# Compression products in native fp32, four kernel rows on four 128x32 column tiles of the array, folded by one matmul

## The chip, the cores and the metric

The kernel runs on one NeuronCore of a Trainium2 chip. The time is the device time of one execution in microseconds (us), and a version is judged by the median of several runs. A NeuronCore has a matrix engine (TensorE, PE in the profile, with its weight loads shown apart as PEld), three engines for elementwise work (VectorE or DVE, ScalarE or ACT, GpSimd or POOL), and SyncE (SP), which here issues the loads of the weights. Each engine works through its own list of instructions in order and meets the others at semaphores.

## The reference

Two blocks run one after the other on 256 tokens of width 2048, everything in fp32. The first mixes a gated delta rule with block attention, the second mixes a compressed, a selected and a windowed attention. Nearly all the arithmetic is in large projections. The change touches one small part of the second block, the compression of keys and values:

```
def _compress(kv, pos_emb, w1, w2):            # kv: 256 tokens, 2 heads, 128 wide
    n_c = (S - CMP_BLOCK) // CMP_STRIDE + 1    # 15 blocks of 32 tokens, every 16
    idx = jnp.arange(n_c)[:, None] * CMP_STRIDE + jnp.arange(CMP_BLOCK)[None, :]
    blocks = kv[:, idx] + pos_emb[None, None, :, None, :]
    flat = blocks.transpose(0, 1, 3, 2, 4).reshape(B, n_c, Hkv, CMP_BLOCK * D)
    return jax.nn.silu(flat @ w1) @ w2         # w1: 4096 x 256, w2: 256 x 128
```

For the keys and again for the values, 30 rows (15 blocks of 2 heads) of length 4096 are multiplied with a matrix of 4096 x 256. Those 4096 are 32 "kernel rows" (the position in the block) of 128 numbers each.

## The kernel before

All weights are streamed once. They are cut into 396 pieces of 128 x 1024 fp32 (512 KB), and one piece is one *tick* of the program. SP loads a piece into one of five buffers `raw_w`. ACT rounds it to the reduced format fp32r (`hi_w`, `split` at L792) and DVE subtracts that from the original (`lo_w`, L1128); both do this two ticks ahead of the matmuls. PE (`products`, L1649) then multiplies in three passes of fp32r: high by high, high by low, low by high. A normal piece gives 12 matmuls with 512 moving columns (L1698). SP loads into a `raw_w` buffer once DVE has made the low part of its former piece (L621).

Between two pieces every engine does the small steps that a table (`PLAN`) puts at that tick: `rope_flip` transposes rotated queries or keys on PE and ACT copies them out, `att` n=0 makes scores, n=1 and 2 the softmax on DVE and ACT, n=3 transposes it on PE (copied by ACT, `att_p`), n=4 multiplies with the values. PE therefore alternates between a piece and a step.

The compression has 16 pieces of its own, eight for the keys (ticks 303, 305, 307, 309, 311, 313, 314, 315) and eight for the values (319, 321, 323, 325, 327, 329, 330, 331), each put between the normal pieces of a query projection. Such a piece holds four kernel rows of the 4096 x 256 matrix. The blocks with their position added (`blk`, L1511) are the stationary operand here and were also split once (`blocks_split`, L1038 and L1524) into `blk_parts`: high and low side by side, 60 columns. For each kernel row there are two matmuls with 256 moving columns (L1669), one of 60 stationary columns against `hi_w` and one of 30 against `lo_w`, all into the same 60 partitions of the accumulator. `cmp_rows` (L1043) copies these 60 rows out, `cmp_fold` (L1930) adds the two halves and transposes them with matmuls against a piece of the identity (L1936), and ACT applies silu to the result (L1050), which makes it load another function table, and another again for the exponentials of `att` that follow.

Of the kernel before, what the change touches and what calls it, by code (L numbers as in the profile page):

```python
# [152 lines left out]
def plan():  # L153
# [113 lines left out]
    for n, part in enumerate("kv"):  # L267
        at(END[("kcv",)] + 5 + n, "blocks", part)
        at(END[("kcv",)] + 6 + n, "blocks_split", part)
        at(END[("cmp", part)] + 1, "cmp_rows", part)  # L270
        at(END[("cmp", part)] + 2, "cmp_fold", part)
        at(END[("cmp", part)] + (6 if part == "k" else 4), "cmp_out", part)
# [41 lines left out]
def constants():  # L314

    i, j = np.arange(P)[:, None], np.arange(P)[None, :]
    f = np.float32
    out = {"ident": (i == j).astype(f), "upto": (i <= j).astype(f)}
    level = []
    for n in range(1, LEVELS + 1):  # L320
        m = 2 ** (n - 1)

        level.append(((i // (2 * m) == j // (2 * m)) & (j // m % 2 == 1) & (i // m % 2 == 0)).astype(f))
    below = (i > j).astype(f)
    out["levels"] = np.ascontiguousarray(np.stack([below, level[0].T] + level, 1))
    causal = np.where(j <= i, 0.0, NEG).astype(f)
    out["masks"] = np.ascontiguousarray(np.concatenate(
        [np.zeros((P, P), f), causal, np.where(j > i, 0.0, NEG).astype(f), causal], 1))
    s = np.arange(SEQ)
    ok = (np.arange(N_CMP) * 16 + 31)[None, :] <= s[:, None]  # L330
    cm = np.stack([np.where(ok, 0.0, NEG), ok.astype(f)], 1).astype(f)
    out["cmask"] = np.ascontiguousarray(cm.reshape(NT, P, 2, N_CMP).transpose(1, 2, 0, 3))
    rope = []
    for d in (128, 64):
        inv = f(10000.0) ** (-np.arange(0, d, 2, dtype=f) / f(d))
        ang = (s.astype(f)[:, None] * inv[None, :].astype(f)).astype(f).astype(np.float64)
        cos, sin = np.cos(ang), np.sin(ang)
        both = np.stack([np.concatenate([cos, cos], 1), np.concatenate([-sin, sin], 1)], 0).astype(f)
        rope.append(both.reshape(2, NT, P, d).transpose(2, 0, 1, 3))
    out["rope_a"], out["rope_b"] = (np.ascontiguousarray(r) for r in rope)  # L340
    return out


def build(nc, known, ins, out):

    ctx = ExitStack()
    with ctx:  # L347
# [29 lines left out]
        levels = place("levels", [P, LEVELS + 2, P], F32)  # L377
        masks = place("masks", [P, 2, SEQ], F32)
        cmask = place("cmask", [P, 2, NT, N_CMP], F32)
        rope_a = place("rope_a", [P, 2, NT, 128], F32)  # L380
# [98 lines left out]
        ob_tok = arena("ob_tok", [P, NT, 16 * 64], F32, 68)  # L479
        blk_parts = {p: arena(f"blk_parts_{p}", [P, CMP_L, 2, 2 * N_CMP], F32R, 16 + 8 * i) for i, p in enumerate("kv")}  # L480
        cmp_rows = arena("cmp_rows", [4 * N_CMP, 256], F32, 32)
        blk = {p: arena(f"blk_{p}", [P, CMP_L, 2, N_CMP], F32, 76 + 4 * i) for i, p in enumerate("kv")}
        qb_t = [arena(f"qb_t{i}", [P, QUAD, SEQ], F32, (8, 76)[i]) for i in range(2)]
# [121 lines left out]


        @block.sync
        def _(sp):
# [8 lines left out]
            def load(no):  # L617
                if no >= RAW_SLOTS:
                    old = no - RAW_SLOTS

                    sp.wait_ge(*lo_ready.after(old))  # L621
                sp.dma_start(piece_view(raw_w[no % RAW_SLOTS], no), piece_source(no)).then_inc(
                    *raw_ready[no % RAW_SLOTS].event(no))
# [12 lines left out]
            for n, (to, source) in enumerate(loads):  # L636
# [3 lines left out]
                (masks[:], ins["masks"].rearrange("p (a b) -> p a b", a=2)),  # L640
                (cmask[:], ins["cmask"]),
                (rope_a[:], ins["rope_a"]),
                (rope_b[:], ins["rope_b"]),
# [140 lines left out]
        def _(act):  # L784
# [7 lines left out]
            def split(no):  # L792

                slot = no % SPLIT_SLOTS
                act.wait_ge(*raw_ready[no % RAW_SLOTS].after(no))
                if no >= SPLIT_SLOTS:
                    act.wait_ge(*used.after(no - SPLIT_SLOTS))
                n = PIECES[no][2] * GROUPS[PIECES[no][0]].cols
                act.activation(hi_w[slot][:, 0:n], raw_w[no % RAW_SLOTS][:, 0:n], ACT.Copy).then_inc(  # L799
                    *hi_ready.event(no))  # L800
# [236 lines left out]

            def blocks_split(part):  # L1038
                act.wait_ge(*dve_did.after("blocks", part))
                act.activation(blk_parts[part][:, :, 0], blk[part][:].rearrange("p l i c -> p l (i c)"),  # L1040
                               ACT.Copy).then_inc(*act_did.event("blocks_hi", part))

            def cmp_rows_(part):  # L1043
                a = acc_of(END[("cmp", part)])
                act.wait_ge(*used.after(END[("cmp", part)]))
                if part == "v":
                    act.wait_ge(*pe_did.after("cmp_fold", "k"))
                act.activation(cmp_rows[:], a[0:4 * N_CMP, 0, 0:256], ACT.Copy).then_inc(*act_did.event("cmp_rows", part))

# [48 lines left out]
            for n in range(2):  # L1098
                for t in range(NT):
# [7 lines left out]
                     "gate_out": gate_out, "y_out": y_out, "head_gates": head_gates,  # L1107
                     "rope": rope, "rope_flip": rope_flip, "blocks_split": blocks_split, "cmp_rows": cmp_rows_,
                     "cmp_fold": cmp_fold, "cmp_out": cmp_out, "catt": catt,
# [10 lines left out]
        def _(dve):  # L1120
# [7 lines left out]
            def split(no):  # L1128

                slot = no % SPLIT_SLOTS  # L1130
                dve.wait_ge(*hi_ready.after(no))
# [63 lines left out]
            def ba_split():  # L1195
                dve.wait_ge(*act_did.after("ba_hi"))
                dve.tensor_tensor(ba_parts[:, :, 1], ba_raw[:, :, 0:16], ba_parts[:, :, 0].bitcast(F32),
                                  ALU.subtract).then_inc(*dve_did.event("ba_lo"))
                dve.wait_ge(*block2_rows.after(8))

# [310 lines left out]
            def blocks(part):  # L1511
# [4 lines left out]
                dve.wait_ge(*act_did.after("rope_flip", "kcv"))  # L1516
                s = kt2["kc" if part == "k" else "vc"][:].rearrange("p i (c l) -> p l i c", l=16)
                for n in range(2):
                    for i in range(2):
                        last = dve.tensor_tensor(blk[part][:, n * 16:(n + 1) * 16, i], s[:, :, i, n:n + N_CMP],  # L1520
                                                 over_cols(pos[part][:, n * 16:(n + 1) * 16], N_CMP), ALU.add)
                last.then_inc(*dve_did.event("blocks", part))

            def blocks_split(part):  # L1524
                dve.wait_ge(*act_did.after("blocks_hi", part))
                dve.tensor_tensor(blk_parts[part][:, :, 1], blk[part][:].rearrange("p l i c -> p l (i c)"),
                                  blk_parts[part][:, :, 0].bitcast(F32), ALU.subtract).then_inc(
                    *dve_did.event("blocks_lo", part))

# [56 lines left out]
            for n in range(2):  # L1586
                for t in range(NT):
# [8 lines left out]
                     "branch": branch, "y_out": y_out, "residual": residual, "head_gates": head_gates, "rope": rope,  # L1596
                     "blocks": blocks, "blocks_split": blocks_split, "catt": catt, "y_gate": y_gate, "y2_out": y2_out, "finish": finish}
            for tick in range(TICKS + LAST):
# [8 lines left out]
        def _(pe):  # L1607
# [41 lines left out]
            def products(no):  # L1649
# [8 lines left out]
                if group.kind == "cmp":  # L1658

                    hi, lo = (piece_view(w[no % SPLIT_SLOTS], no) for w in (hi_w, lo_w))  # L1660
                    parts = blk_parts[group.name[1]]
                    pe.wait_ge(*lo_ready.after(no))
                    pe.wait_ge(*dve_did.after("blocks_lo", group.name[1]))
                    for k in range(k0, k0 + n):
                        at_end = last and k == k0 + n - 1
                        both = ((4 * N_CMP, parts[:, k].rearrange("p b c -> p (b c)"), hi),
                                (2 * N_CMP, parts[:, k, 0], lo))
                        for m, (rows, x, w) in enumerate(both[::-1] if at_end else both):
                            i = pe.matmul(to[0:rows, 0, 0:256], x, w[:, k - k0], start=first and k == k0 and m == 0,  # L1669
                                          stop=at_end and m == 1)  # L1670
                    i.then_inc(*used.event(no))
# [258 lines left out]
            def cmp_fold(part):  # L1930
# [3 lines left out]
                for m in range(2):  # L1934
                    for b in range(2):
                        last = pe.matmul(aux[:, 0, m * 2 * N_CMP:(m + 1) * 2 * N_CMP], cmp_rows[:, m * P:(m + 1) * P],  # L1936
                                         ident[0:4 * N_CMP, b * 2 * N_CMP:(b + 1) * 2 * N_CMP], start=b == 0,
                                         stop=b == 1)
                last.then_inc(*pe_did.event("cmp_fold", part))
# [99 lines left out]
```

## Time and profile before

| | |
|---|---|
| median of 3 runs | 1315.29 us (1315.05 to 1315.99) |
| profiled execution, its own time | 1316.64 us |
| its span | 1314.8 us |
| PE busy | 1255.6 us, 95% of the span |
| PEld busy | 1085.6 us, 83% |
| DVE busy | 761.7 us, 58% |
| ACT busy | 615.5 us, 47% |
| PE, DVE, ACT busy from 1003.6 to 1091.3 us (the stretch of the compression pieces) | 84.2, 62.6, 53.4 of 87.7 us |

Busy time counts an instruction from its start to its end, and consecutive matmuls overlap: what a matmul costs is the distance from its start to that of the next. A native fp32 matmul stands in the trace as two records with a weight load each, an fp32r matmul as one. "128\*60 128x256" is a matmul with 128 rows and 60 columns of stationary operand and 256 moving columns.

### The profile page before, as it was taken

Reading aid. Unit: us, or ns where it says so; the run is one execution under the profiler, and the core shown is the slowest. Engines: PE = TensorE matmul, PEld = TensorE weight load, DVE = VectorE, ACT = ScalarE, POOL = GpSimd, SP = SyncE. Lnnn points to the kernel's source line nnn. Section 1 sums busy time; section 2 is a strip of 40 time slices with the busy share of each in tenths; the row PEclk is TensorE's granted clock in tenths of the full one; section 3 lists DMA queues with packets and bytes.
Section 4 is the critical chain, followed back from the end, with each engine's and each line's share of the span. In section 5 each row is a group of like instructions: output and inputs, shape, how many; then the busy total and the mean of one; then the engine's idle time right before and its main releaser. Section 6 shows DMA issues by size and latency. Waiting matters only on the chain. (4 is left out here: it accounts for less than half of the span.)

```text
span 1314.8 us, 17365 instructions
## 1 busy us (share of the span) xinstructions
PE 1255.6 (95%) x7040; PEld 1085.6 (83%) x7040; DVE 761.7 (58%) x976; ACT 615.5 (47%) x869; POOL 89.5 (7%) x126
## 2 busy tenths in 40 slices
PE   8999999995999999999999999799999999999996
PEld 6999988995988888888888888678888787878885
DVE  5668775652556646546454555477566766465553
ACT  4555445432223545543434344254445555466443
POOL 0100001197000000000000000000000000000000
PEclk9999999998999999999999999899999999999998
DMA  8646554563334654555566595355545655454662
GB/s 273 188 129 192 163 190 139 163 205 103 114 96 118 202 160 129 189 193 184 190 191 192 191 325 185 120 192 179 179 140 162 191 161 156 133 201 160 213 197 78
DMA packets 120705, 225.60 MB, mean 172 GB/s; under 512 B 9825, under 2 KB 21505, under 8 KB 119473
## 3 DMA queue, kind: packets, MB, share of 16 engines
q1 hardware_dynamic: 118386, 213.81, 51.7%
q0 software_dynamic: 2240, 10.68, 2.3%
q8 instruction: 56, 0.92, 0.3%
q14 instruction: 23, 0.19, 0.0%
HBM read 219.75 MB, written 4.72 MB: 171 GB/s over the span
## 5 line engine op out<-in xcount | busy, mean ns | idle before, releaser
L1133 DVE TENSOR_TENSOR lo_w<-raw_w,hi_w 128x1024 fp32r<-128x1024 f32 x396 | 482.1, 1229 | 373.5 <-ACT hi_w L799 372.3
L799 ACT ACTIVATE hi_w<-raw_w 128x1024 fp32r<-128x1024 f32 x396 | 411.1, 1057 | 263.5 <-PE acc L1698 208.0
L1698 PE MATMUL acc<-hi_w,h_hi 128*128 128x512 f32 (+1 forms) x832 | 330.9, 398 | 3.0 <-DVE h_lo L1141 2.7
L1698 PE MATMUL acc<-hi_w,h_lo 128*128 128x512 f32 (+1 forms) x832 | 322.2, 387 | 0.0
L1698 PE MATMUL acc<-lo_w,h_hi 128*128 128x512 f32 (+1 forms) x832 | 321.7, 387 | 0.0
L1689 PE MATMUL acc<-h_hi,hi_w 128*128 128x256 f32 x640 | 185.1, 289 | 1.3 <-DVE lo_w L1133 1.3
L1698 PEld LDWEIGHTS acc<-hi_w,h_hi 128*128 128x128 f32 x832 | 157.0, 189 | 34.8 <-issue 5.0
L1698 PEld LDWEIGHTS acc<-hi_w,h_lo 128*128 128x128 f32 x832 | 156.9, 189 | 32.5
L1689 PE MATMUL acc<-h_lo,hi_w 128*128 128x256 f32 x640 | 182.3, 285 | 0.0
L1689 PE MATMUL acc<-h_hi,lo_w 128*128 128x256 f32 x640 | 182.2, 285 | 0.0
L1698 PEld LDWEIGHTS acc<-lo_w,h_hi 128*128 128x128 f32 x832 | 157.2, 189 | 30.0 <-issue 0.7
L1689 PEld LDWEIGHTS acc<-h_hi,hi_w 128*128 128x128 f32 x640 | 124.1, 194 | 1.7 <-issue 1.6
L1689 PEld LDWEIGHTS acc<-h_lo,hi_w 128*128 128x128 f32 x640 | 124.2, 194 | 0.1
L1689 PEld LDWEIGHTS acc<-h_hi,lo_w 128*128 128x128 f32 x640 | 124.0, 194 | 0.0
L1698 PE MATMUL acc<-hi_w,m_hi 128*128 128x512 f32 x256 | 99.8, 390 | 0.0
L1698 PE MATMUL acc<-hi_w,m_lo 128*128 128x512 f32 x256 | 99.6, 389 | 0.0
L1698 PE MATMUL acc<-lo_w,m_hi 128*128 128x512 f32 x256 | 99.6, 389 | 0.0
L1698 PEld LDWEIGHTS acc<-hi_w,m_lo 128*128 128x128 f32 x256 | 48.0, 188 | 10.0
L1698 PEld LDWEIGHTS acc<-hi_w,m_hi 128*128 128x128 f32 x256 | 48.1, 188 | 9.9
L1698 PEld LDWEIGHTS acc<-lo_w,m_hi 128*128 128x128 f32 x256 | 48.1, 188 | 9.9
L954 ACT ACTIVATE att_s<-att_s,small 128x128 f32<-128x128 f32 (+1 forms) x80 | 35.5, 446 | 15.0 <-DVE small L1391 14.8
L1234 DVE SCALAR_TENSOR_TENSOR cv<-raw,conv_w,cv 128x255 f32<-128x255 f32 (+2 forms) x72 | 31.5, 479 | 3.9 <-ACT cv L861 3.0
(324 smaller groups left out, 1220.7 us busy)
## 6 DMA issues: line engine op xcount, KB each, us to landing
raw_w<-in_w_in SPq DMA_DIRECT2D x284, 512.0 KB, 3.7
raw_w<-in_w_out SPq DMA_DIRECT2D x64, 512.0 KB, 4.7
raw_w<-in_w_branch_a SPq DMA_DIRECT2D x16, 512.0 KB, 4.6
raw_w<-in_w_branch_b SPq DMA_DIRECT2D x16, 512.0 KB, 4.6
raw_w<-in_cmp_k_w SPq DMA_DIRECT2D x8, 512.0 KB, 4.4
raw_w<-in_cmp_v_w SPq DMA_DIRECT2D x8, 512.0 KB, 4.2
x_in<-in_x SPq DMA_DIRECT2D x4, 512.0 KB, 5.9
x<-in_x POOLq DMA_DIRECT2D x1, 2048.0 KB, 10.7
```

The source lines that it names most:

```text
L799: act.activation(hi_w[slot][:, 0:n], raw_w[no % RAW_SLOTS][:, 0:n], ACT.Copy).then_inc(*hi_ready.event(no))
L954: e = act.activation(att_s[:, i * k:(i + 1) * k], att_s[:, i * k:(i + 1) * k], ACT.Exp, bias=nmx[:, i:i + 1], scale=sc, accum_out=den[:, i ...
L1133: dve.tensor_tensor(lo_w[slot][:, 0:n], raw_w[no % RAW_SLOTS][:, 0:n], hi_w[slot][:, 0:n].bitcast(F32), ALU.subtract).then_inc(*lo_ready.e ...
L1234: last = dve.scalar_tensor_tensor(cv[:, i, back:SEQ], raw[:, i, 0:SEQ - back], conv_w[:, CONV - 1 - back, first + i:first + i + 1], cv[:, ...
L1689: i = pe.matmul(channels_of(no)[:, c], w[:, k, c * P:(c + 1) * P], x[:, k0 + k], start=first and c % 2 == 0 and k == 0 and m == 0, stop=la ...
L1698: i = pe.matmul(to[:, t, 0:group.cols], x[at], w[:, k], start=first and k == 0 and m == 0, stop=last and k == n - 1 and m == 2)
```

## The change

The compression pieces are no longer split, on ACT nor on DVE. PE multiplies the loaded `raw_w` itself in native fp32. The stationary operand is `blk`, now 32 columns per kernel row (30 and two of zeros), and kernel row k of a piece writes to the partitions 32k to 32k+31 of the accumulator, which places it on the k-th of four column tiles of the array. After eight pieces the 128 partitions hold four partial sums; `cmp_rows` copies 128 rows instead of 60, and `cmp_fold` adds the four and transposes them in one native matmul per half against a constant matrix `fold`. The buffer of such a piece becomes free when PE has used it, since no split reads it. `blocks_split` goes, on ACT and DVE.

```
-        at(END[("kcv",)] + 6 + n, "blocks_split", part)
...
+    out["fold"] = np.ascontiguousarray((i % 32 == np.arange(2 * N_CMP)[None, :]).astype(f))
...
+        def whole(no):
+            return GROUPS[PIECES[no][0]].kind == "cmp"
...
-                    sp.wait_ge(*lo_ready.after(old))
+                    sp.wait_ge(*(used if whole(old) else lo_ready).after(old))
...
+                (fold[:, 0:2 * N_CMP], ins["fold"]),
...
             def split(no):
+                if whole(no):
+                    return
...
-                act.activation(cmp_rows[:], a[0:4 * N_CMP, 0, 0:256], ACT.Copy).then_inc(*act_did.event("cmp_rows", part))
+                act.activation(cmp_rows[:], a[:, 0, 0:256], ACT.Copy).then_inc(*act_did.event("cmp_rows", part))
...
+                dve.memset(blk[part][:, :, 2 * N_CMP:32], 0.0)
...
-                    hi, lo = (piece_view(w[no % SPLIT_SLOTS], no) for w in (hi_w, lo_w))
-                    parts = blk_parts[group.name[1]]
-                    pe.wait_ge(*lo_ready.after(no))
-                    pe.wait_ge(*dve_did.after("blocks_lo", group.name[1]))
-                    for k in range(k0, k0 + n):
-                        at_end = last and k == k0 + n - 1
-                        both = ((4 * N_CMP, parts[:, k].rearrange("p b c -> p (b c)"), hi),
-                                (2 * N_CMP, parts[:, k, 0], lo))
-                        for m, (rows, x, w) in enumerate(both[::-1] if at_end else both):
-                            i = pe.matmul(to[0:rows, 0, 0:256], x, w[:, k - k0], start=first and k == k0 and m == 0,
-                                          stop=at_end and m == 1)
+                    w = piece_view(raw_w[no % RAW_SLOTS], no)
+                    pe.wait_ge(*raw_ready[no % RAW_SLOTS].after(no))
+                    pe.wait_ge(*dve_did.after("blocks", group.name[1]))
+                    for k in range(n):
+                        i = pe.matmul(to[32 * k:32 * (k + 1), 0, 0:256], blk[group.name[1]][:, k0 + k], w[:, k],
+                                      start=first, stop=last)
...
                 for m in range(2):
-                    for b in range(2):
-                        last = pe.matmul(aux[:, 0, m * 2 * N_CMP:(m + 1) * 2 * N_CMP], cmp_rows[:, m * P:(m + 1) * P],
-                                         ident[0:4 * N_CMP, b * 2 * N_CMP:(b + 1) * 2 * N_CMP], start=b == 0,
-                                         stop=b == 1)
+                    last = pe.matmul(aux[:, 0, m * 2 * N_CMP:(m + 1) * 2 * N_CMP], cmp_rows[:, m * P:(m + 1) * P],
+                                     fold[:, 0:2 * N_CMP], start=True, stop=True)
```

On PE, at the first compression piece of the keys (tick 303, between the transposes of `rope_flip` and the scores of `att`), the list of instructions read before:

```order
L1617 MATMUL aux<-ident,rot_165 128x128 x8
L1669 MATMUL acc<-hi_w_57,blk_parts_k 60x256
L1669 MATMUL acc<-lo_w_61,blk_parts_k 30x256
L1669 MATMUL acc<-hi_w_57,blk_parts_k 60x256
L1669 MATMUL acc<-lo_w_61,blk_parts_k 30x256
L1669 MATMUL acc<-hi_w_57,blk_parts_k 60x256
L1669 MATMUL acc<-lo_w_61,blk_parts_k 30x256
L1669 MATMUL acc<-hi_w_57,blk_parts_k 60x256
L1669 MATMUL acc<-lo_w_61,blk_parts_k 30x256
L1881 MATMUL aux<-kz,qb_t_161 128x256 x2
L1698 MATMUL acc<-hi_w_54,h_hi 128x512
```

and reads now (the sizes are those of the output):

```order
L1617 MATMUL aux<-ident,rot_164 128x128 x8
L1664 MATMUL acc<-raw_w_52,blk_k 32x256 x4
L1876 MATMUL aux<-kz,qb_t_160 128x256 x2
L1693 MATMUL acc<-hi_w_54,h_hi 128x512
```

Eight fp32r matmuls became four native ones, with the same neighbours on both sides.

On ACT, from the copy of `rope_flip` for `qb` at tick 302 to the copy of `att_p` two steps later, the list read before:

```order
L1027 ACTIVATE qb_t0_161<-aux 128x1024
L799 ACTIVATE hi_w1_55<-raw_w0_49 128x1024
L799 ACTIVATE hi_w2_56<-raw_w1_50 128x1024
L799 ACTIVATE hi_w3_57<-raw_w2_51 128x1024
L952 ACTIVATE small_74<-small_74 128x4
L954 ACTIVATE att_s_126,small_74<-att_s_126,small_74 128x128 x4
L799 ACTIVATE hi_w0_54<-raw_w3_52 128x1024
L961 ACTIVATE att_p_127<-aux 128x512
```

and reads now:

```order
L1034 ACTIVATE qb_t0_160<-aux 128x1024
L806 ACTIVATE hi_w2_56<-raw_w1_50 128x1024
L959 ACTIVATE small_75<-small_75 128x4
L961 ACTIVATE att_s_127,small_75<-att_s_127,small_75 128x128 x4
L806 ACTIVATE hi_w0_54<-raw_w3_52 128x1024
L968 ACTIVATE att_p_128<-aux 128x512
```

The two splits of compression pieces (`raw_w0`, `raw_w2`) are gone from ahead of the exponentials; DVE loses the matching two subtractions.

## Rows read from the trace of the kernel before

**Rows 1.** The page: engines; costliest groups (busy us, mean ns | idle before); loads (us to landing).

```profile
PE 1255.6 (95%) x7040; PEld 1085.6 (83%) x7040; DVE 761.7 (58%) x976; ACT 615.5 (47%) x869; POOL 89.5 (7%) x126
...
L1133 DVE TENSOR_TENSOR lo_w<-raw_w,hi_w 128x1024 fp32r<-128x1024 f32 x396 | 482.1, 1229 | 373.5 <-ACT hi_w L799 372.3
L799 ACT ACTIVATE hi_w<-raw_w 128x1024 fp32r<-128x1024 f32 x396 | 411.1, 1057 | 263.5 <-PE acc L1698 208.0
...
raw_w<-in_w_in SPq DMA_DIRECT2D x284, 512.0 KB, 3.7
```

**Rows 2.** Timeline of PE at tick 305 (start us, us from first start to last end).

```profile
1012.29 0.28 PE L1669 MATMUL acc<-hi_w,blk_parts_k 128*60 128x256 f32 x1
1012.41 0.28 PE L1669 MATMUL acc<-lo_w,blk_parts_k 128*30 128x256 f32 x1
...
1013.24 0.40 PE L1698 MATMUL acc<-hi_w,h_hi 128*128 128x512 f32 x1
```

**Rows 3.** Line L1669 alone (count: ns min/median/max, first and last start us).

```profile
L1669 PE MATMUL acc<-hi_w,blk_parts_k x32: 276/280/361, 1007.1 to 1037.7; 128*60 128x256 f32 x32
```

**Rows 4.** Groups by form on PE from 1007 to 1089 us: a native matmul of 256 columns.

```profile
L1888 PE MATMUL aux<-ks_t,qa_t 128*128 128x256 f32 x8 | 1.9, 379 | 0.0
```

**Rows 5.** Timeline around the fold of the values.

```profile
1096.84 1.03 PE L1617 MATMUL aux<-ident,rot 128*128 128x128 f32 x8
...
1097.80 1.07 PE L1936 MATMUL aux<-ident,cmp_rows 60*128 60x30 f32 x8
...
1098.81 0.50 PE L1698 MATMUL acc<-hi_w,h_hi 128*128 128x512 f32 x1
...
1099.14 0.39 PE L1698 MATMUL acc<-lo_w,h_hi 128*128 128x512 f32 x1
```

**Rows 6.** Timeline around the second compression matmul of the values (15 stationary columns).

```profile
1107.75 1.05 PE L1950 MATMUL aux<-w_v,hs_v 128*15 128x128 f32 x8
1108.72 0.41 PEld L1912 LDWEIGHTS aux<-vw_tok,att_p 128*128 128x128 f32 x3 [0.21 <-issue]
1108.73 0.49 PE L1912 MATMUL aux<-vw_tok,att_p 128*128 128x128 f32 x2
```

**Rows 7.** Waits of PE from 1007 to 1092 us (total us, times, longest).

```profile
PE aux L1617 <- ACT att_s L954: 2.5, 2, 2.3
PE aux L1912 <- ACT att_p L961: 0.4, 2, 0.2
PE aux L1881 <- ACT qb_t L1027: 0.3, 1, 0.3
PE acc L1698 <- DVE lo_w L1133: 0.2, 1, 0.2
```

**Rows 8.** Timeline of PE behind the piece of tick 311.

```profile
1028.23 0.28 PE L1669 MATMUL acc<-lo_w,blk_parts_k 128*30 128x256 f32 x1
1028.70 0.99 PE L1912 MATMUL aux<-vb,att_p 128*128 128x64 f32 x7 [0.19 <-ACT att_p L961]
```

**Rows 9.** Timeline: ACT from the copy of `rope_flip`, and PE's next transposes.

```profile
1047.39 1.02 ACT L1027 ACTIVATE qa_t<-aux 128x1024 f32<-128x1024 f32 x1 [6.53 <-PE aux L1617]
...
1048.43 1.28 ACT L1052 ACT_TABLE_LOAD   x1
...
1053.58 1.28 PE L1617 MATMUL aux<-ident,att_s 128*128 128x128 f32 x8 [2.27 <-ACT att_s L954]
```

**Rows 10.** The same transposes behind the values' fold.

```profile
1104.01 1.07 PE L1617 MATMUL aux<-ident,att_s 128*128 128x128 f32 x8 [2.19 <-ACT att_s L954]
```

**Rows 11.** Busy time by stretch: after the columns of the engines PEclk, DMA share, GB/s.

```profile
1054.30:1057.70 3.40, 3.40 (x19) 3.22 (x17) 2.02 (x2) 2.89 (x4) 0.00 (x0) 0.50 0.20 40
1104.00:1107.40 3.40, 3.39 (x19) 2.98 (x20) 1.51 (x2) 2.79 (x3) 0.00 (x0) 1.00 0.10 16
```

**Rows 12.** Timeline: load of tick 310 and the splits of 309 to 311.

```profile
1010.66 0.37 SPq L622 DMA_DIRECT2D raw_w<-in_w_in  x1
...
1017.10 2.94 ACT L799 ACTIVATE hi_w<-raw_w 128x1024 fp32r<-128x1024 f32 x3
```

More of the change, by code:

```diff
@@ L378, in build @@
         masks = place("masks", [P, 2, SEQ], F32)
+        fold = place("fold", [P, 32], F32)
         cmask = place("cmask", [P, 2, NT, N_CMP], F32)
@@ L479, in build @@
         ob_tok = arena("ob_tok", [P, NT, 16 * 64], F32, 68)
-        blk_parts = {p: arena(f"blk_parts_{p}", [P, CMP_L, 2, 2 * N_CMP], F32R, 16 + 8 * i) for i, p in enumerate("kv")}
-        cmp_rows = arena("cmp_rows", [4 * N_CMP, 256], F32, 32)
-        blk = {p: arena(f"blk_{p}", [P, CMP_L, 2, N_CMP], F32, 76 + 4 * i) for i, p in enumerate("kv")}
+        cmp_rows = arena("cmp_rows", [P, 256], F32, 32)
+        blk = {p: arena(f"blk_{p}", [P, CMP_L, 32], F32, 76 + 4 * i) for i, p in enumerate("kv")}
         qb_t = [arena(f"qb_t{i}", [P, QUAD, SEQ], F32, (8, 76)[i]) for i in range(2)]
@@ L1036, in rope_flip @@
                 i.then_inc(*act_did.event("rope_flip", *name))
[L1038 to L1041, printed above, removed]
             def cmp_rows_(part):
@@ L1107, in _ @@
                      "gate_out": gate_out, "y_out": y_out, "head_gates": head_gates,
-                     "rope": rope, "rope_flip": rope_flip, "blocks_split": blocks_split, "cmp_rows": cmp_rows_,
+                     "rope": rope, "rope_flip": rope_flip, "cmp_rows": cmp_rows_,
                      "cmp_fold": cmp_fold, "cmp_out": cmp_out, "catt": catt,
@@ L1128, in split @@
             def split(no):
+                if whole(no):
+                    return
                 slot = no % SPLIT_SLOTS
@@ L1198, in ba_split @@
                                   ALU.subtract).then_inc(*dve_did.event("ba_lo"))
-                dve.wait_ge(*block2_rows.after(8))
+                dve.wait_ge(*block2_rows.after(9))
             def r1_row_():
@@ L1517, in blocks @@
                 s = kt2["kc" if part == "k" else "vc"][:].rearrange("p i (c l) -> p l i c", l=16)
+                dve.memset(blk[part][:, :, 2 * N_CMP:32], 0.0)
                 for n in range(2):
                     for i in range(2):
-                        last = dve.tensor_tensor(blk[part][:, n * 16:(n + 1) * 16, i], s[:, :, i, n:n + N_CMP],
+                        to = blk[part][:, n * 16:(n + 1) * 16, i * N_CMP:(i + 1) * N_CMP]
+                        last = dve.tensor_tensor(to, s[:, :, i, n:n + N_CMP],
                                                  over_cols(pos[part][:, n * 16:(n + 1) * 16], N_CMP), ALU.add)
                 last.then_inc(*dve_did.event("blocks", part))
[L1524 to L1528, printed above, removed]
             def catt(t, n):
@@ L1596, in _ @@
                      "branch": branch, "y_out": y_out, "residual": residual, "head_gates": head_gates, "rope": rope,
-                     "blocks": blocks, "blocks_split": blocks_split, "catt": catt, "y_gate": y_gate, "y2_out": y2_out, "finish": finish}
+                     "blocks": blocks, "catt": catt, "y_gate": y_gate, "y2_out": y2_out, "finish": finish}
             for tick in range(TICKS + LAST):
```

## Prediction

> **What bounds the kernel now.** I read the page first: PE is busy for 95% of the span, DVE 58% and ACT 47% [rows 1], so a microsecond taken from DVE or ACT counts only where PE waits for it. Next I read PE's timeline at one compression piece. The reader is to see distances between starts, not durations: eight matmuls of 256 columns follow each other every 0.118 us, from 1012.29 to the next piece's start at 1013.24, 0.95 us in all, and nothing is lost at either edge [rows 2]. There are 64 such matmuls for the keys (32 high, and as many low) and 64 for the values [rows 3], so the 16 pieces hold PE for about 15 us. Last I read PE's waits in this stretch: 3.4 us in six waits, of which 2.3 is one long one behind the fold of the keys [rows 7], and a like one of 2.19 us follows the fold of the values [rows 10]. All waits but the long one follow a compression piece or a normal piece whose `lo_w` came late. The idle column counts from the modelled end of the last matmul, so the delay is larger than it says: behind tick 311 the starts are 0.47 us apart where 0.12 is usual, a loss of 0.35 [rows 8]. Read so (start to start, in the same timeline), the five waits behind compression pieces (ticks 303, 311, 314, 327, 330) cost 0.43, 0.35, 0.38, 0.35 and 0.23 us, and the two for `lo_w` (ticks 316 and 332) about 0.35 each; the waits view leaves out the last of the five and the first of the two, since their idle part is under its threshold.
>
> **Streaming of a piece.** The nearest row for a native fp32 matmul of 256 columns is L1888: eight records take 1.9 us from first start to last end and one lasts 0.379, so they start every (1.89 - 0.38)/7 = 0.216 us [rows 4], using 1.89 from the timeline that rounds to this 1.9. Two records are one matmul, 0.43 us, against 0.118 for a pass of fp32r. A changed piece has four native matmuls, eight records. What a piece costs then hangs on how far the column tiles work at the same time, which no row of this trace shows: every matmul here writes from partition 0 on. The bounds are: one after the other, 8 x 0.216 = 1.73 us; all four tiles at once, 2 x 0.216 and a few ns, 0.44 us. Between these lies what I expect. PE starts its matmuls in the order of its list, and the two records of one native matmul use the same tile and stand next to each other. The second must wait 0.216 us for the first; the next tile's first record can start beside it, but that tile's second must wait again. So the records pair up like stairs, five steps of 0.216 = 1.08 us. I take this, +0.13 us per piece, 16 pieces, **+2.1 us**.
>
> By the Trainium skill (TensorE: Matmul & The Clock Gate, Part 3) matmuls start and end strictly in program order, and a group packed on several tiles spans one matmul plus about 4 ns per tile. The first half gives my stairs; the second, read without regard to the two records, gives 0.44 us per piece and the rival below.
>
> **Going to the tiles and back.** Where PE changes from a full-size matmul to one on part of the array, the trace shows a price. Into the fold (60 of 128 rows) the starts are 0.96 us apart for eight records of 0.109 us, 0.09 too long; its own eight take 1.01 us at 0.112 each, 0.1 too long by its end; and the matmul behind it has its successor 0.33 us later where 0.23 is usual, 0.1 more [rows 5]. With 15 of 128 columns in native fp32 it is the same: 0.98 us for eight records of 0.109, and the weight load behind it could not run ahead (idle 0.21) [rows 6]. So one round trip costs 0.3 us. The old 60- and 30-column matmuls in fp32r paid none [rows 2]. The 16 pieces make 14 round trips, since nothing of PE's stands between ticks 313 and 314, nor 329 and 330: **+4.2 us**.
>
> The Trainium skill (TensorEngine Tiling (Array Packing), Key Properties) says that a change of tiling mode drains TensorE; the rows above give the price.
>
> **Waits that absorb.** The five waits behind compression pieces end with ACT's copy or exponential, not with PE. PE comes there 0.13 + 0.19 us later (the longer piece, the way in, and the drain), so it waits 0.32 less, or down to nothing: 4 x 0.32 + 0.23 = **-1.5 us**. (At 1.73 us per piece they vanish, -1.75; at 0.44 they grow by 0.32 each, +1.6.)
>
> **Relief of DVE and ACT.** Sixteen splits go: 16 x 1.06 = 17 us of ACT and 16 x 1.23 = 20 us of DVE [rows 1]. PE waited for `lo_w` twice with a loss of 0.35 each, behind three compression pieces in a row: **-0.7 us**. The rest was hidden behind PE and is worth nothing. `blocks_split`, 1.0 us on ACT and 1.2 on DVE twice, lies under unbroken projection matmuls of `qa`, as do the two small memsets that come instead.
>
> **The fold.** Half of its records go and it now uses all 128 rows: 0.45 + 0.3 = 0.75 us less of PE, twice. But behind it PE has one normal piece and then waits for an exponential whose chain on ACT begins with the copy of `rope_flip` before the fold and goes straight on: the copy ends at 1048.41 and the table load starts at 1048.43, silu, table, exponentials [rows 9]. The fold, finished by 1048.4, is no later than that copy. So PE's 2.27 us become 3.0, and 2.19 become 2.9 [rows 9, 10]: 0. That is if the clock stays. Behind the first of these gaps the granted clock was 0.50 for 3.4 us, which is the 1.2 GHz level, behind the second it was 1.00 [rows 11]; half speed for 3.4 us costs 1.7. With longer gaps it may fall behind both or neither, +-1.7 us in the range, 0 in the sum.
>
> **Loads.** A `raw_w` buffer of a compression piece is now freed by PE and not by DVE, some 2.5 us later, and SP's queue is in order, so every later load waits too. Tightest is tick 310: its load went at 1010.66, and would go when PE ends tick 305, at 1013.24; with 3.7 us to landing [rows 1] that is 1016.9. ACT split tick 310 as the second of three at 1018.1 [rows 12], so 1.1 us remain, and PE took the piece only at 1023.7, 5.6 us later than ACT. Cost 0. The one added constant takes half a microsecond of SP's queue at the start, ahead of a load that landed two microseconds before ACT took it: 0.
>
> **Sum.** 2.1 + 4.2 - 1.5 - 0.7 = +4.1 us on the profiled execution's 1316.64, 1320.7. The profiled one stands 1.35 above the median of the runs; on that median, 1315.29, it is **1319.4 us**, +0.31%.
>
> **Rivals.** All go by the same sum with another streaming time.
> (1) All four tiles at once, 0.44 us a piece: 16 x (-0.51) = -8.2, +4.2, +1.6, -0.7 = -3.1, **1312.2 us**. For it: the order of starts alone doesn't forbid it if the tiles' two records can wait independently. Against it: the adjacent records of one matmul stand 0.216 apart in every row. The sum crosses zero at about 0.72 us per piece; below that the kernel is faster.
> (2) No overlap: native fp32 on column tiles runs one after the other, so the change doesn't do what it says: 16 x 0.78 = 12.5, +4.2, -1.75, -0.7 = +14.2, **1329.5 us**. For it: in every row of native fp32 a record starts only when the one before has streamed.
> (3) Stairs, and the clock falls behind both gaps: +4.1 + 1.7, **1321.1 us**. Longer idle speaks for it, one of two gaps without a fall against.
> (4) Loads come late after all: if landing took over 6 us in the stretch, ACT would split later by 1 us at some ticks. DVE and ACT have over 5 us of lead over PE there, so 1321 at most.
>
> **How the numbers follow.** Stairs at a steady clock count 0.34, and with (3) and (4) 0.44; (2) 0.28; (1) 0.23; something else 0.05. A difference under 0.2% (2.6 us) cannot be told from no change on this kernel. Stairs lie above that except where the clock gets better (0.08 of the 0.44 go to same). (1) at -0.24% sits on the edge, half faster and half same. So faster 0.14, same 0.22, slower 0.64. The range goes from (1) to (2), since leaving either out would leave out more than 2 in 10: 1312 to 1330. The stairs' own range is 1317.5 to 1321.5.
>
> **What would show it.** Starts of the eight records within a piece: pairs a few ns apart every 0.216 us (right), all in two bunches (1), or an even 0.216 (2). From first record to the next full-size matmul: 1.17 us, and 0.1 more behind it. Waits for `qb_t`, `att_p` and `att_s` behind compression pieces near zero, none for `lo_w` at ticks 316 and 332, the two long gaps at 2.9 to 3.0 us. I am wrong if a round trip costs much less than 0.3 with column tiles, or if the tiles don't pair.

## The result, and the profile after

The changed kernel takes **1318.5 us** (median of 20 runs, 1316.9 to 1322.02), the kernel before 1316.26 us in the same comparison (20 runs, 1314.62 to 1318.1): ratio **1.002**, 95% interval 1.0013 to 1.0026. The forecast was 1319.4 us. The number is nearly right; the difference is less so: +4.1 us was forecast and +2.2 us measured (interval 1.7 to 3.4), and the kernel before is itself 1.0 us above the median on which the forecast stands. The sum behind the number is wrong in two places that work against each other: the stretch where the change works got faster, about as the forecast's rival (1) says, and matmuls that the change never mentions got slower.

The profiled execution of the changed kernel took 1322.02 us, span 1319.8; it is the longest of its 20 runs, so sizes below are taken from distances between starts, not from its end.

First the place of the change. PE's timeline at one compression piece (tick 305), which answers to [rows 2]:

```profile
1019.36 0.39 PE L1693 MATMUL acc<-hi_w,h_lo 128*128 128x512 f32 x1
1019.68 0.64 PE L1664 MATMUL acc<-raw_w,blk_k 128*32 128x256 f32 x8
1020.25 0.50 PE L1693 MATMUL acc<-hi_w,h_hi 128*128 128x512 f32 x1
1020.59 0.39 PE L1693 MATMUL acc<-lo_w,h_hi 128*128 128x512 f32 x1
```

The piece's eight records fill 0.64 us from first start to last end, where one alone lasts 0.38 to 0.40. The same piece as a group of its own records (count: ns min/median/max, first and last start us):

```profile
L1664 PE MATMUL acc<-raw_w,blk_k x8: 379/391/403, 1019.7 to 1019.9; 128*32 128x256 f32 x8
```

All eight start between 1019.7 and 1019.9. In the single records there are two bunches: 1019.68, .69, .70, .70, and then 1019.92, .93, .94, .94. That is the first pass of all four column tiles, 6 to 7 ns apart, and 0.24 us later the second pass of all four. The next full-size matmul starts 0.57 us after the first record, where the forecast said 1.17 and the old piece took 0.95. The price of going to the tiles and back stands beside it as forecast: 1019.36 to 1019.68 is 0.32 where 0.23 is usual, 1020.25 to 1020.59 is 0.34 where 0.23 is usual, and 0.57 less the 0.46 of streaming leaves 0.11: 0.3 us.

PE's waits from 1000 to 1115 us, for [rows 7] and [rows 10]:

```profile
PE aux L1617 <- ACT att_s L961: 5.9, 2, 3.0
PE aux L1907 <- ACT att_p L968: 1.6, 3, 0.5
PE aux L1876 <- ACT qb_t L1034: 0.6, 1, 0.6
```

The two long gaps are 3.0 and 2.9 us, `lo_w` is gone from the list, and the waits for `att_p` and `qb_t` grew instead of vanishing, because PE comes there earlier. Between the start of tick 303 and that of tick 332 the changed kernel gains 4.5 us on the one before (from 1014.61 to 1094.30 us, against 1007.13 to 1091.27). Not all of that is the change. In the kernel before, a fall of the granted clock to 0.50 [rows 11] covers the piece of tick 319 and the step behind it; from the start of the piece to that of the scores behind the step it takes 4.23 us there:

```profile
1054.51 0.56 PE L1669 MATMUL acc<-hi_w,blk_parts_v 128*60 128x256 f32 x1
1058.74 1.11 PE L1888 MATMUL aux<-ks_t,qa_t 128*128 128x128 f32 x8
```

and 3.19 us in the last kernel of the experiments below, which has the same piece and step at a granted clock of 1.00:

```profile
1052.55 0.36 PE L1671 MATMUL acc<-hi_w,blk_parts_v 128*60 128x256 f32 x1
1055.74 1.11 PE L1890 MATMUL aux<-ks_t,qa_t 128*128 128x128 f32 x8
```

So about 1.0 of the 4.5 us is the clock, and some 3.4 us are left for the change.

Now matmuls that the change doesn't touch, those of 512 columns as groups (busy us, mean ns of one | idle before). The second name is the tile held in the array, the stationary operand. In the kernel before:

```profile
L1698 PE MATMUL acc<-hi_w,h_lo 128*128 128x512 f32 x800 | 313.1, 391 | 0.0
L1698 PE MATMUL acc<-hi_w,m_hi 128*128 128x512 f32 x256 | 99.8, 390 | 0.0
L1698 PE MATMUL acc<-hi_w,ob_hi 128*128 128x512 f32 x64 | 24.9, 389 | 0.0
```

And after:

```profile
L1693 PE MATMUL acc<-hi_w,h_lo 128*128 128x512 f32 x800 | 314.2, 393 | 0.0
L1693 PE MATMUL acc<-hi_w,m_hi 128*128 128x512 f32 x256 | 101.2, 395 | 0.0
L1693 PE MATMUL acc<-hi_w,ob_hi 128*128 128x512 f32 x64 | 25.3, 395 | 0.0
```

Each record from `m` and `ob` lasts 5 to 6 ns longer. Records overlap, so the distance between starts decides: in PE's timeline at the last projection, twelve matmuls take 2.72 us before (1290.05 to 1292.77):

```profile
1290.05 0.39 PE L1698 MATMUL acc<-hi_w,m_hi 128*128 128x512 f32 x1
...
1292.77 0.39 PE L1698 MATMUL acc<-hi_w,m_hi 128*128 128x512 f32 x1
```

and 2.79 us after (1290.02 to 1292.81):

```profile
1290.02 0.39 PE L1693 MATMUL acc<-hi_w,m_hi 128*128 128x512 f32 x1
...
1292.81 0.39 PE L1693 MATMUL acc<-hi_w,m_hi 128*128 128x512 f32 x1
```

Over all of them the mean distance is 226.7 ns before and 232.4 ns after. This holds for every matmul of 512 columns whose stationary operand lies in the working area (`oa`, `ob`, `m`: 192 + 192 + 768 = 1152), and for none from `h_hi` or `h_lo`. 1152 x 5.7 ns = **6.6 us**. What the change did to them is one line of the diff: `fold`, 128 bytes a partition, was placed ahead of `cmask`, so that all tiles behind it, the working area too, lie 128 bytes higher, while `hi_w`, `lo_w` and `h` stay.

### The profile page after: what moved, and what is told of

Same layout as the page of the kernel before. It is cut to its first block and busy times, and to the rows that moved or that the text cites. A ratio compares the mean times of both kernels' runs of the same rounds, so it can differ in the third digit from the quotient of the medians.

```text
span 1319.8 us, 17300 instructions
## 1 busy us (share of the span) xinstructions
PE 1256.6 (95%) x7032; PEld 1073.9 (81%) x7032; DVE 741.8 (56%) x960; ACT 598.4 (45%) x851; POOL 89.5 (7%) x126
## 5 line engine op out<-in xcount | busy, mean ns | idle before, releaser
L1137 DVE TENSOR_TENSOR lo_w<-raw_w,hi_w 128x1024 fp32r<-128x1024 f32 x380 | 462.8, 1229 | 381.7 <-ACT hi_w L806 380.3
L806 ACT ACTIVATE hi_w<-raw_w 128x1024 fp32r<-128x1024 f32 x380 | 395.6, 1056 | 279.1 <-PE acc L1693 221.9
```

The lines of the kernel that those rows point to most:

```text
L1137: dve.tensor_tensor(lo_w[slot][:, 0:n], raw_w[no % RAW_SLOTS][:, 0:n], hi_w[slot][:, 0:n].bitcast(F32), ALU.subtract).then_inc(*lo_ready.e ...
```

## The experiments

Kernels that went to the same chip share its runs of the kernel before, whose median there was 1316.27, 1317.47 and 1315.65 us for the three groups below. Ratios are to those, with 95% intervals.

### Where the lost time is

The changed kernel with the constant somewhere else:

```diff
-        fold = place("fold", [P, 32], F32)
...
+        fold = arena("fold", [P, 32], F32, 106.5)
```

> The changed kernel, with its constant `fold` placed above the working area (at 106.5 KB from its start), so that nothing else moves from where it was before the change. Placement theory: the 1152 matmuls of 512 columns whose stationary operand lies in the working area (oa, ob, m) start 226.7 ns apart again and not 232.4, 1152 x 5.7 ns = 6.6 us, so 1318.5 - 6.6 = 1311.9 us, below both kernels; their records last 389 to 390 ns and not 395. Rival, that the time is lost in the pieces, their round trips or the clock and not by the placement: 1318.5 us, records still 395 ns.

Measured: 1313.51 us (12 runs), ratio 0.9979 (0.9967 to 0.9991); 5.0 us less than the changed kernel (5.4 by the two ratios) for moving one constant, where 6.6 were expected. The records are back at

```profile
L1693 PE MATMUL acc<-hi_w,m_hi 128*128 128x512 f32 x256 | 99.8, 390 | 0.0
```

and the distance at 226.7 ns. The placement theory holds, and the change without its side effect is faster than the kernel before by 2.8 us (interval 1.2 to 4.3). Part of this can be the clock: the mean granted clock of its 12 runs is 0.9850, that of the 29 runs of the kernel before 0.9838, and 0.0012 of 1316 us is 1.6 us, an estimate of the most that it can be. Then the reverse, the shift without the change:

```diff
+        place("unused", [P, 32], F32)
         cmask = place("cmask", [P, 2, NT, N_CMP], F32)
```

> The kernel before, with an unused tile of 128 bytes a partition ahead of `cmask`, so that the working area moves by 128 bytes and nothing else changes. Placement theory: 1316.3 + 6.6 = 1322.9 us, the matmuls from oa, ob and m at 232.4 ns, those from h_hi and h_lo at 226.7. Rival (placement is free): 1316.3 us.

Measured: 1324.92 us (5 runs), ratio 1.0058 (1.0045 to 1.0071), 8.7 us more between the medians and 7.6 by the ratio, interval 5.9 to 9.3. The matmuls from `m` take the same step:

```profile
L1699 PE MATMUL acc<-hi_w,m_hi 128*128 128x512 f32 x256 | 101.2, 395 | 0.0
```

Their mean distance is 232.4 ns. Those from `h` stay at 227.4 to 228.0, which they have in the kernel before too. Two more falls of the clock than in the profile of the kernel before (3.4 us at half speed each, at 393.8 and 1110.6) may be the rest of the 8.7. Next 256 bytes (`[P, 64]` in the same place), and then all tiles moved together:

> The kernel before, with the working area moved by 256 bytes. If the place within 256 bytes counts: 1316.3 us, all at 226.7 ns. If any other distance from the weights' buffers or a larger period counts: about 1322.9 us or more.

Measured: 1317.17 us (11 runs), ratio 1.0003 (0.9994 to 1.0011); 226.7 ns. The second:

```diff
-        cursor = [start]
+        cursor = [start + 128]
```

> The kernel before, with every tile moved by 128 bytes, the weights' buffers too, so that no distance between two operands changes. If the distance between the stationary and the moving operand counts: 1316.3 us, all at 226.7 ns. If the place of one operand by itself counts: the 2400 matmuls of 512 columns from h_hi and h_lo slow down too, 3552 x 5.7 ns = 20.2 us, 1336.5 us, and up to 5.5 us more if the 1920 matmuls of 256 columns lose half as much each.

Measured: 1316.48 us (11 runs), ratio 1.0001 (0.9992 to 1.0009); all at 226.7 ns. So moving everything costs nothing, and 128 bytes cost what 256 bytes do not: what counts is how far operands lie apart, counted modulo 256 bytes (in the kernel before, the buffers, `h` and the working area all start at multiples of 256 bytes from one another). Then 64 bytes (`[P, 16]`):

> The kernel before with its working area moved by 64 bytes. 0 and 256 bytes cost nothing, 128 bytes 8.6 us. If the cost grows evenly with the distance to the next multiple of 256: half, about 1320.6 us, starts 229.6 ns apart. If only the 128-byte half counts: 1316.3 or 1324.9 us. If any misfit costs the same: 1324.9 us.

Measured: 1324.73 us (6 runs), ratio 1.0055 (1.0039 to 1.007); distance 233.4 ns. Half the shift costs no less than the whole, so the cost does not grow with it. Last, one of the four kinds of operand alone:

```diff
+        place("unused0", [P, 32], F32)
         lo_w = [place(f"lo_w{i}", [P, PIECE_KT * COLS], F32R) for i in range(SPLIT_SLOTS)]
+        place("unused1", [P, 32], F32)
```

> The kernel before, with the four `lo_w` buffers alone moved by 128 bytes (all behind them by 256). If the misfit is one between the two operands of a matmul: those of `lo_w` with h_hi, oa_hi and m_hi alone go from 226.7 to about 232.4 ns, 1184 x 5.7 = 6.7 us, 1323.5 us or some more if the 640 of 256 columns lose too; those of `hi_w` stay at 226.7. If it is one of the working area with something else (transfers into `raw_w`, the writes of ACT and DVE): no matmul changes, about 1316.8 us.

Measured: 1332.06 us (4 runs), ratio 1.0121 (1.0106 to 1.0135). The rival is out, since now the matmuls from `h` slow down as well; but my size was wrong by more than two, because the cost does not stay with the matmuls of `lo_w`. PE's timeline in a projection from `h`:

```profile
900.11 0.40 PE L1700 MATMUL acc<-hi_w,h_lo 128*128 128x512 f32 x1
900.34 0.39 PE L1700 MATMUL acc<-hi_w,h_hi 128*128 128x512 f32 x1
900.57 0.39 PE L1700 MATMUL acc<-lo_w,h_hi 128*128 128x512 f32 x1
...
902.88 0.40 PE L1700 MATMUL acc<-hi_w,h_lo 128*128 128x512 f32 x1
```

Twelve distances make 2.77 us, 231 ns each. Over the whole trace those that end at a start of `lo_w,h_hi`, `hi_w,h_lo` and `hi_w,h_hi` are 234.1, 232.5 and 230.9 ns, where the kernel before has 227.8, 227.4 and 227.9: 14.4 ns for three, 11.5 us for 800 such threes. The 384 threes from `oa`, `ob` and `m` lose 16.6 to 19.9 ns each, some 6.8 us. That makes 18 us; the runs say 16.4, interval 13.9 to 17.8. The 1920 matmuls of 256 columns lose nothing: their distances go from 119.8 to 119.1 ns, which gives back 1.3 us. Each of the three neighbours in the list is touched, so the misfit is not one of a matmul's own two operands only. Which pair of reads collides stays open.

### What the column tiles do

All four kernel rows on one column tile, `fold` on top:

```diff
-                        i = pe.matmul(to[32 * k:32 * (k + 1), 0, 0:256], blk[group.name[1]][:, k0 + k], w[:, k],
-                                      start=first, stop=last)
+                        i = pe.matmul(to[0:32, 0, 0:256], blk[group.name[1]][:, k0 + k], w[:, k],
+                                      start=first and k < 1, stop=last and k >= 3)
```

(The copy and the fold then take 32 rows.)

> The changed kernel with `fold` on top (1313.5 us), and all four kernel rows of a piece on the first column tile, summed in PSUM. If different tiles overlap and one tile does not: 8 x 0.216 = 1.73 us of streaming a piece instead of 0.46, 16 x 1.27 = 20.3 us, less some 3.3 us of waits behind pieces that vanish, so 1330.5 us, with eight even starts 0.216 us apart. Rival, that the bunches come from the 32 columns alone and not from the four tiles: 1313.5 us with bunches as before.

Measured: 1331.57 us (4 runs), ratio 1.0111 (1.0092 to 1.0129). Starts within the piece are 0.215 to 0.217 us apart, behind a first distance of 0.24. With two column tiles (`to[32 * (k % 2):...]`, kernel rows 2 and 3 added to 0 and 1):

> As the run before, but kernel rows 0 and 2 on the first column tile, 1 and 3 on the second. If the tiles run at once and one tile's records one after the other: four bunches of two, 4 x 0.216 = 0.88 us a piece, 16 x 0.42 = 6.7 us, less about 2 us of waits that shrink: 1318.2 us. If the order of the list holds (stairs): pairs of the second pass of one with the first pass of the next, seven steps or so, 1.3 us a piece or more, 1325 us.

Measured: 1319.23 us (10 runs), ratio 1.0016 (1.0004 to 1.0028). The three pieces side by side, each behind transposes of `att_s` or `rot`; one tile, then two, then four:

```profile
1016.62 1.91 PE L1664 MATMUL acc<-raw_w,blk_k 128*32 128x256 f32 x8
```

```profile
1015.00 1.06 PE L1664 MATMUL acc<-raw_w,blk_k 128*32 128x256 f32 x8
```

```profile
1017.88 0.64 PE L1664 MATMUL acc<-raw_w,blk_k 128*32 128x256 f32 x8
```

Less one record's 0.38 these are 1.53, 0.68 and 0.26 us from first to last start. With two tiles the records start at 1005.54, .54, then .78, .78, then .99, 1006.00, then 1006.21, .22: four bunches of two. The two passes of one matmul wait for each other, and so do two matmuls on one tile; matmuls on different tiles start 7 ns apart. The stairs of the forecast are in no trace.

The price of a round trip by itself. The run with one column tile, but as a full-size matmul:

```diff
-                        i = pe.matmul(to[0:32, 0, 0:256], blk[group.name[1]][:, k0 + k], w[:, k],
+                        i = pe.matmul(to[:, 0, 0:256], blk[group.name[1]][:, k0:k0 + n].rearrange("p k c -> p (k c)"), w[:, k],
```

> As the run with one column tile (1331.6 us), but each matmul takes all four kernel rows of the piece as a stationary operand of 128 columns and writes 128 partitions, so that the same eight records of 256 columns run on the full array (the sums then mix kernel rows: this changes what is computed). If the price of 0.3 to 0.4 us a round trip is that of column tiles: 14 x 0.4 = 5.6 us less, 1326 us, starts into and out of a piece at usual distances. If it is that of native fp32 behind fp32r: 1331.6 us.

Measured: 1325.69 us (4 runs), ratio 1.0072 (1.0059 to 1.0086). From the start of tick 303 to that of 332 it takes 4.3 us less than the run with one column tile, with one fall of the clock in each: 4.3 / 14 = 0.30 us a trip. Its piece and what follows:

```profile
1018.23 0.60 PE L1617 MATMUL aux<-ident,att_s 128*128 128x128 f32 x4
1018.66 1.89 PE L1664 MATMUL acc<-raw_w,blk_k 128*128 128x256 f32 x8
1020.39 1.00 PE L1907 MATMUL aux<-vb,att_p 128*128 128x64 f32 x8
```

Four transposes take 0.43 us to the piece and the piece 1.73 to the next matmul; with one column tile it is 0.52 and 1.85:

```profile
1016.10 0.60 PE L1617 MATMUL aux<-ident,att_s 128*128 128x128 f32 x4
1016.62 1.91 PE L1664 MATMUL acc<-raw_w,blk_k 128*32 128x256 f32 x8
1018.47 0.77 PE L1907 MATMUL aux<-vb,att_p 128*128 128x64 f32 x5
```

So native fp32 itself costs nothing to go to; using 32 of the 128 columns does. (The matmuls of the kernel before with 60 and 30 columns, in fp32r, paid nothing [rows 2], so the price is shown for native fp32 only.) In the single records the way in takes 0.203 us with one column tile and 0.109 at full width, the next matmul starts 0.310 us behind the piece's last record against 0.215, and its successor comes up to 0.11 late.

### What the fold's shortening is worth

In both kernels the fold's gain was hidden by the long gaps, which end with exponentials behind two table loads and a silu on ACT. So I moved those away, with `fold` on top:

```diff
-        at(END[("cmp", part)] + 2, "cmp_fold", part)
+        at(END[("cmp", part)] + 3, "cmp_fold", part)
...
+    for part in "kv":
+        at(END[("cmp", part)] + 3, "cmp_silu", part)
...
-                     "cmp_fold": cmp_fold, "cmp_out": cmp_out, "catt": catt,
+                     "cmp_silu": cmp_fold, "cmp_out": cmp_out, "catt": catt,
```

(The last two lines are in ACT's table of steps; the new step is planned behind those of the attention, so that ACT takes it after the tick's copy of `att_p`.)

> The changed kernel with `fold` on top (1313.5 us), and each part's fold one tick later on PE, its silu on ACT behind that tick's copy of `att_p`, so that the two table loads and the silu (2.8 us) no longer stand ahead of the exponentials that PE waits for. If the two long gaps (3.0 and 2.9 us) are these: both go to near zero, 1313.5 - 5.9 = 1307.6 us. Rival: the silu now holds the bank that the next scores take, or the table loads hold the next copy, and the wait comes back there: 1310 to 1313.5 us.

Measured: **1306.87 us** (5 runs, 1305.73 to 1307.9), ratio 0.9918 (0.9903 to 0.9933), the fastest of all. ACT's timeline:

```profile
1049.78 1.02 ACT L970 ACTIVATE att_p<-aux 128x1024 f32<-128x1024 f32 x1 [0.30 <-PE aux L1619]
1050.82 1.28 ACT L1056 ACT_TABLE_LOAD   x1
1052.12 0.22 ACT L1056 ACTIVATE hs_k<-aux 128x60 f32<-128x60 f32 x1
```

and PE's:

```profile
1048.00 0.52 PE L1932 MATMUL aux<-fold,cmp_rows 128*128 128x30 f32 x4
1048.68 1.06 PE L1619 MATMUL aux<-ident,att_s 128*128 128x128 f32 x8 [0.16 <-ACT att_s L963]
```

The gap of 3.0 us is 0.16, and the one behind the values' fold is 0.05. A smaller one came in their place: the second table load now stands ahead of the exponentials of a later tick (at 1057.96 us, behind `ck_t`), and PE waits for those:

```profile
1061.05 0.63 PE L1619 MATMUL aux<-ident,att_s 128*128 128x128 f32 x4 [0.53 <-ACT att_s L963]
```

The normal piece ahead of it takes 3.50 us from its start to these transposes, where it takes 2.82 in the run with `fold` on top. So the rival was right for 0.7 us. In the traces, from tick 303 to tick 336, the edit gains 5.2 us (98.99 to 93.84), which is the forecast 5.9 less this 0.7. The medians differ by more, 6.6 us, but they are from two chips. The same edit in the kernel before:

> The kernel before with the same move of the fold and the silu as in the run that took 1306.9 us, and nothing else. If the change's fold (0.75 us shorter, twice) was worth nothing only because the long gaps hid it, it now counts: this kernel is 3.1 + 1.5 = 4.6 us slower than that one, 1311.5 us. If the fold is hidden by something else as well: 1310 us.

Measured: 1311.29 us (6 runs), ratio 0.9966 (0.9953 to 0.9978). From tick 303 to tick 336 it takes 98.78 us, the one with column tiles 93.84; the clock falls in neither. The 4.9 us between them are near the 4.6 expected, but not all of it is what was expected. One wait stands in this kernel alone, at the step behind the piece of tick 321, where VectorE is late with the scores' maximum:

```profile
1061.05 0.63 PE L1949 MATMUL aux<-hs_k,w_k 128*128 128x30 f32 x4 [0.50 <-DVE small L1393]
```

It costs 0.66 us from start to start (the piece takes 1.61 to the next step instead of 0.94). The two folds are worth 1.0 us here and not 1.5: each is over 0.7 us shorter, but PE then comes to the exponentials before they are done, and 0.41 us of the first and 0.55 of the second count. That leaves 3.3 us for the pieces, their round trips and waits. So the fold's gain was indeed hidden by the long gaps, for two thirds of its size, and that the sum came out at 4.6 is partly luck.

## Why the prediction was right or wrong

**Streaming of a piece (+2.1 us): wrong, the step that failed first.** I wrote that the second record of a native matmul must wait 0.216 us and that "the next tile's first record can start beside it, but that tile's second must wait again", hence five steps. The waiting is as said, but it is the tile's own: the first passes of all four tiles go out 7 ns apart, before the second pass of any. Two steps, 0.24 us between the bunches as measured and 0.22 for the second to stream (the distance of one record to the next in the run with one tile), make 0.46 and not 1.08: **-7.8 us** in place of +2.1. The rows I argued from all had consecutive records on the full array, where the two rules look the same. By the Trainium skill (TensorE: Matmul & The Clock Gate, Part 3) a packed group spans one matmul plus about 4 ns a tile; the trace agrees, with 6 to 7 ns, and I gave the reading from the list's order more weight than this one, which was rival (1) with a chance of 0.23.

**Round trips (+4.2 us): right.** 14 x 0.30, measured by the run at full width against the one at 32 columns.

**Waits that absorb (-1.5 us): wrong in sign, and only because streaming was.** For 0.44 us a piece the prediction had +1.6. The waits for `att_p` and `qb_t` behind pieces went from 0.7 us in [rows 7] to 2.2 (from 1000 to 1115 us the kernel before has 0.7 too). The modelled ends hide more: with `fold` on top, the piece that starts at 1017.88 is followed at 1018.64, 0.76 us later, by a matmul that needs ACT's copy, which ends at 1018.59, and the idle column shows nothing. From start to start in the changed kernel (a piece without a wait takes 0.57 us to the next matmul, two in a row 1.00) the five waits that the forecast names cost 0.71, 0.62, 0.17, 0.62 and 0, together 2.1 us where they cost 1.7, and four more pieces (ticks 307, 315, 323, 331) take 0.19 to 0.21 us longer than 0.57. That is about +1.2 us.

**Relief of `lo_w` (-0.7 us): right in direction, and mis-sized.** Both ticks still start late; only the idle parts fell below what the waits view lists. The start of tick 332 comes 0.48 us behind the last record of the step before it, and it was 0.57:

```profile
1093.83 0.38 PE L1883 MATMUL aux<-kw_t,qa_t 128*128 128x256 f32 x1
1094.30 0.47 PE L1693 MATMUL acc<-hi_w,h_hi 128*128 128x512 f32 x1
```

(before: 1090.70 and 1091.27 us). `lo_w` of this piece is done at 1094.17 us, 0.13 before that start. At tick 316 the same distance went from 0.70 to 0.54. That is 0.25 us gained in all.

**The fold (0): right, and the reason shown.** The gaps are the forecast 3.0 and 2.9 us. With ACT's table loads out of the way the two folds are worth 1.0 us.

**Loads (0): right, with less to spare than I said.** The load of tick 310 went out at 1020.38, and ACT split it at 1024.35, right behind its landing at 1024.33; PE took the piece at 1030.51, 6.2 us later.

**Clock (0 in the sum): within the 1.7 us allowed, and to the good.** Where the granted clock was 0.50 behind the keys' gap in [rows 11], it is 1.00 behind both gaps now (stretch, then PE, PEld, DVE, ACT and POOL busy, PEclk, DMA share, GB/s):

```profile
1059.26:1062.70 3.44, 2.90 (x27) 2.25 (x28) 1.48 (x3) 2.77 (x3) 0.00 (x0) 1.00 0.19 35
1107.03:1110.50 3.47, 3.47 (x20) 2.97 (x20) 1.59 (x2) 2.77 (x3) 0.00 (x0) 1.00 0.11 16
```

although the gaps grew. That is the 1.0 us above. All five profiles of the kernel before or of it merely shifted by 64 to 256 bytes show one or two such falls of 3.4 us between 1050 and 1115 us, as does the run with `lo_w` moved; none of the three profiles with four column tiles does, but neither does that of the kernel before with fold and silu moved. Two of these four have no long gap left, so there no fall is missing. In the other two, the changed kernel and the one with `fold` on top, a gap of 3.0 us is followed by none, and why stays open. In the profiled execution of the changed kernel the clock also stood at half for 6.8 us from 392.5, which the one before has not (392 to 400 us, PEclk 0.57):

```profile
392.00:400.00 8.00, 7.51 (x26) 6.39 (x27) 4.45 (x6) 0.00 (x0) 1.30 (x2) 0.57 0.18 53
```

A fall of 3.4 us at this place (392 to 394 us) stands in the profiles of three of the shifted or edited versions of the kernel before, too, so it is not the change that makes the clock fall there. At half speed 6.8 us cost up to 3.4 us, about the 3.5 by which that execution is above its median; that this is the whole reason is not shown.

**The missing term (+6.6 us).** The change part by part ended, in the prediction, with what each operation costs. One edit was costed by its transfer alone: "the one added constant takes half a microsecond of SP's queue at the start ... 0". It also moved every tile behind it. The sum as it should have been: rival (1), -3.1, plus 6.6, makes +3.5 us, and +2.2 was measured. On 1315.29, the median that the forecast had, this gives 1318.8 us; on 1316.26, the median of the comparison, 1319.8, against 1318.5 measured. The 1.3 us are not accounted for. The kernel with the constant on top, -3.1 on 1316.27 = 1313.2, took 1313.51. In rival (1) itself two terms are off by half a microsecond and in opposite directions: the waits cost 1.2 and not 1.6, `lo_w` gives 0.25 and not 0.7.

So the forecast's side (slower, 0.64) came true for a cause that was in none of its cases, and the likeliest mechanism was the wrong one: that the number fits is luck. By the forecast's own mark, 2.6 us, the 2.2 us would even have counted as no change.

## What to carry to other kernels

A constant added ahead of other tiles is an edit of all of them: compare the addresses of both versions, keep the operands of TensorE at one distance modulo 256 bytes, and put new small tiles at the end. Small matmuls that go to different column tiles run at the same time in native fp32 too, both passes bunched, so count passes per tile and not per list, and add 0.3 us for each return to the full array. A gain that lands in front of a wait set by another engine can be had once that wait is moved; here the move by itself (4.4 us in the kernel before) was worth more than the change (2.8). And read distances between starts before calling a wait gone or a gain the change's own: a short wait drops out of the list, and a fall of the clock in one of two traces looks like a gain in the other.

## What the runs showed of the hardware

- Matmuls of 512 columns in fp32r: 226.7 ns from start to start with all operands at one distance modulo 256 bytes, 232.4 ns with the stationary ones 128 bytes off, 233.4 with 64, 226.7 with 256; 230 to 236 with one of the two moving operands 128 off. Those of 256 columns, where `h` moves and the weights are stationary, lost nothing then (119.8 and 119.1 ns).
- Native fp32 on column tiles: tiles start 6 to 7 ns apart, the second passes 0.22 to 0.24 us after the first; 1.53, 0.68 and 0.26 us from first to last start for the same eight records on one, two and four tiles.
- In native fp32, going from the full array to a 32-column tile and back costs 0.30 us, of it 0.09 on the way in; native fp32 on the full array behind fp32r costs nothing.
